# A fourth weight buffer for the experts, and scatters that add into a running sum in memory

## The reference: what is computed

```python
def hier_moe(h, w_rg, b_rg, w_re, b_re, w_eg, w_eu, w_ed):
    ...                       # softmax over 4 groups, the best group g_sel; 8 experts in it, the best 2
    weights = pg_top * pe_top                      # (T, 2)
    gidx = g_sel * EXPERTS_PER_GROUP + e_sel       # both experts of a token are in one group
    ...
    for e in range(N_EXPERTS):                     # 32 experts, FF = 256
        a = jax.nn.silu(h @ w_eg[e]) * (h @ w_eu[e])
        out = out + gate[:, e:e + 1] * (a @ w_ed[e])
    return out
...
hm = rmsnorm(x, norm_moe)
x = x + hier_moe(hm, ...)
return rmsnorm(x, norm_final)
```

## Time and profile before

| | |
|---|---|
| median of 3 runs | 1280.27 us (1277.06 to 1283.28) |
| the profiled execution | 1284.23 us, its span 1282.5 us |
| the experts' tiles | about 921 to 1244 us of the span |
| the end behind them | 1244 to 1282.5 us |
| PE busy | 1185.2 us, 92% of the span |
| moved by DMA | 184.53 MB, of these 100.7 MB expert weights (96 loads of 1 MB) |

### The profile page before, as it was taken

How to read it: one execution, slowest core, us unless ns; L and a number is a source line. 1 busy time by engine, 2 the same in 40 slices (tenths; PEclk the granted TensorE clock), 3 DMA queues, 4 the chain that set the end, 5 groups by cost and what they waited for, 6 DMA issues and landing times.

```text
span 1282.5 us, 18554 instructions
## 1 busy us (share of the span) xinstructions
PE 1185.2 (92%) x7302; PEld 1070.8 (83%) x7302; DVE 643.9 (50%) x1057; ACT 602.7 (47%) x998; POOL 331.8 (26%) x225
## 2 busy tenths in 40 slices
PE   7999999998999999999999999999699999999960
PEld 6999899888878878899999999999687887777750
DVE  4201512436653443355302021435788998888857
ACT  5333644645644444133212213123477887787843
POOL 0221112123203111131112023210244465444520
PEclk9999999998999999999999999999799999999995
DMA  6441101124102021112121222501889999999817
GB/s 221 166 140 34 33 14 42 51 78 120 50 1 68 1 66 34 34 46 60 47 66 42 66 75 66 186 34 39 332 319 374 365 363 348 369 351 363 338 61 295
DMA packets 93575, 184.53 MB, mean 144 GB/s; under 512 B 17385, under 2 KB 68989, under 8 KB 85310
## 3 DMA queue, kind: packets, MB, share of 16 engines
q1 hardware_dynamic: 82606, 167.43, 36.9%
q0 software_dynamic: 10896, 16.08, 3.5%
HBM read 179.72 MB, written 28.65 MB: 162 GB/s over the span
## 4 chain that ended last, share of the span: by engine, by line
PE 71%; ACT 9%; DVE 8%; DMA 6%; issue 4%; SPq 0%; POOL 0%; POOLq 0%; ACTq 0%; DVEq 0%
PE bank L1297 11%; PE bank L1299 11%; PE bank L1298 11%; DMA raw_gu<-in_w_exp_up 5%; PE bank L1364 5%; PE bank L1365 5%; PE bank L1366 5%; PE bank L1498 3%; PE bank L1500 3%; PE bank L1499 3%; PE bank L1445 2%; PE bank L1376 2%; ACT w_hi L1041 1%; PE bank L1398 1%; PE bank L1485 1%
## 5 line engine op out<-in xcount | busy, mean ns | idle before, releaser
L913 POOL TENSOR_TENSOR w_lo<-raw,w_hi 128x2048 fp32r<-128x2048 f32 (+2 forms) x34 | 140.6, 4136 | 598.2 <-ACT w_hi L1041 453.0
L1297 PE MATMUL bank<-hT_hi,w_hi 128*128 128x384 f32 (+1 forms) x592 | 202.6, 342 | 2.5 <-POOL w_lo L913 1.8
L1299 PE MATMUL bank<-hT_hi,w_lo 128*128 128x384 f32 (+1 forms) x592 | 199.6, 337 | 0.0
L1298 PE MATMUL bank<-hT_lo,w_hi 128*128 128x384 f32 (+1 forms) x592 | 199.4, 337 | 0.0
L1931 DVE TENSOR_TENSOR lo_gu<-raw_gu,hi_gu 128x2048 fp32r<-128x2048 f32 x64 | 146.3, 2287 | 4.7 <-ACT hi_gu L1030 4.5
L1030 ACT ACTIVATE hi_gu<-raw_gu 128x2048 fp32r<-128x2048 f32 x64 | 122.5, 1918 | 51.0 <-issue 51.0
L1364 PE MATMUL bank<-w_hi,hT_hi 128*128 128x256 f32 x432 | 124.8, 289 | 0.0
L1365 PE MATMUL bank<-w_lo,hT_hi 128*128 128x256 f32 x432 | 122.1, 283 | 0.0
L1366 PE MATMUL bank<-w_hi,hT_lo 128*128 128x256 f32 x432 | 122.1, 283 | 0.0
L1297 PEld LDWEIGHTS bank<-hT_hi,w_hi 128*128 128x128 f32 (+1 forms) x592 | 112.1, 189 | 6.3 <-issue 5.2
L1298 PEld LDWEIGHTS bank<-hT_lo,w_hi 128*128 128x128 f32 (+1 forms) x592 | 112.1, 189 | 0.3
(11 more groups left out here) (301 smaller groups left out, 2626.0 us busy)
## 6 DMA issues: line engine op xcount, KB each, us to landing
raw_gu<-in_w_exp_gate SPq DMA_DIRECT2D x32, 1024.0 KB, 11.2
raw_gu<-in_w_exp_up SPq DMA_DIRECT2D x32, 1024.0 KB, 13.7
raw_down<-in_w_exp_down SPq DMA_DIRECT2D x32, 1024.0 KB, 15.4
raw<-in_w_in SPq DMA_DIRECT2D x25, 1024.0 KB, 5.6
y_pair<-y_d SPq DMA_DIRECT2D x12, 512.0 KB, 8.5
raw<-in_w_in SPq DMA_DIRECT2D x8, 512.0 KB, 5.5
raw<-in_w_proj_b SPq DMA_DIRECT2D x4, 1024.0 KB, 5.1
raw<-in_w_out SPq DMA_DIRECT2D x4, 1024.0 KB, 5.6
```

Source lines behind the costliest of these rows:

```text
L913: pool.tensor_tensor(w_lo[:, g % 2, 0:kb, 0:n], raw[:, g % 2, 0:kb, 0:n], w_hi[:, g % 2, 0:kb, 0:n].bitcast(F32), ALU.subtract).then_inc(w ...
L1297: pe.matmul(out, l_hi, r_hi, start=j == 0, stop=False)
L1298: pe.matmul(out, l_hi, r_lo, start=False, stop=False)
L1299: ins = pe.matmul(out, l_lo, r_hi, start=False, stop=j == n - 1)
```

## The change

`WRING` is 4: a fourth gate/up buffer and a fourth down buffer stand where `x1` stood (140 to 164 KB of a partition). The loop becomes 2 turns of 12 tiles, since 12 is a multiple of the 4 buffers and the 2 places. `x1` moves to memory: as soon as a tile of tokens has its final x1, SP stores it to `sum_d` (768 x 1024). The result of an expert is scaled by the pair's weight on ACT as it leaves PE's accumulator, and the scatter adds it to the token's row of `sum_d`. For this the table now has a slot's row index alone (`slot_x`) and its weights (`slot_w`), which come from a wider float32 matmul (`w_hot`, 56 columns where there were 24) in the place of the overflow table. Since both experts of a token lie in one group, the tiles take the groups in turn (0, 8, 16, 24, 1, 9, ...), so that two scatters in flight never add to one row. At the end SP loads 6 tiles of `sum_d` and not 12 of `y_d`, and the products and sums of L1991 are gone.

```diff
-WRING = 3
+WRING = 4
...
-        gu_raw = [at(f"raw_gu{r}", [P, 2, KD, FF], F32, kb) for r, kb in enumerate((8, 24, 104))]
+        gu_raw = [at(f"raw_gu{r}", [P, 2, KD, FF], F32, kb) for r, kb in enumerate((8, 24, 104, 140))]
...
-        y_pair = at("y_pair", [P, NT, 2, D], F32, 8)
+        x_sum = at("x_sum", [P, NT, D], F32, 8)
...
-        LOOPED = 4
-        FIRST, TURN = 2, 2 * WRING
+        LOOPED = 2
+        FIRST, TURN = 2, 12
...
+        def expert_at(i, g, n):
+
+            return (g + n) % NGRP * EPG + i + (g + n) // NGRP
...
+                if s.kind == "h2T" and s.half == 0:
+
+                    evac_done(sp, E_, find(kind="ts", dest=("out", 3), i=s.i)[0].job)
+                    sp.dma_start(sum_d[s.i * P:(s.i + 1) * P, :], x1[:, s.i, :]).then_inc(x1_out, 16)
...
-            load(kinds[0:2], 2, 2, 2)
-            sp.wait_ge(over_mm, 1)
+            load(kinds[0:2], expert_at(0, 0, 2), 2, 2)
+            sp.wait_ge(x1_out, 16 * NT)
+            sp.wait_ge(h2_out, 16 * NT)
+            load(kinds[0:2], expert_at(0, 0, 3), 3, 3)
+            sp.wait_ge(w_mm, 1)
+            load(kinds[2:3], expert_at(0, 0, 2), 2, 2)
...
             for i in range(NT):
-                for j in range(2):
-                    sp.dma_start(y_pair[:, i, j, :], y_d[j * T + i * P:j * T + (i + 1) * P, :]).then_inc(pair_in[i], 16)
+                sp.dma_start(x_sum[:, i, :], sum_d[i * P:(i + 1) * P, :]).then_inc(sum_in[i], 16)
...
-            def scatter(e, p, k):
+            def scatter(e, p, k, ring, slot):
...
                     pool.wait_ge(y_out[p], k * 16)
...
+                pool.tensor_copy(y_idx[:, p:p + 1], slot_x[:, bass.ds(slot, 1)]).then_inc(y_copied, 1)
+                pool.tensor_copy(y_w[:, p:p + 1], slot_w[:, bass.ds(slot, 1)]).then_inc(y_copied, 1)
+                pool.wait_ge(y_copied, e * 2 + 2)
                 pool.wait_ge(y_done, e + 1)
                 pool.sem_inc(y_ready, 1)
-                pool.indirect_dma_start(y_d, bass.IndirectOffsetOnAxis(ap=y_idx[:, p:p + 1].bitcast(U32), axis=0),
-                                        m_y[:, p, :], None, bounds_check=2 * T - 1, oob_is_err=False).then_inc(y_out[p], 16)
+                pool.indirect_dma_start(sum_d, bass.IndirectOffsetOnAxis(ap=y_idx[:, p:p + 1].bitcast(U32), axis=0),
+                                        m_y[:, p, :], None, bounds_check=T - 1, oob_is_err=False,
+                                        compute_op=ALU.add).then_inc(y_out[p], 16)
...
+            pool.wait_ge(y_out[1], NE // 2 * 16)
             n_over = beyond(pool, beyond_tile)
             pool.wait_ge(y_out[0], (n_over + NE // 2) * 16)
-            pool.wait_ge(y_out[1], NE // 2 * 16)
...
+                act.wait_ge(y_copied, e * 2 + 2)
...
+                    ins = act.activation(m_y[:, p, half * 512:(half + 1) * 512], psum[B_Y[half]][:, :], ACT.Copy,
+                                         scale=y_w[:, p:p + 1])
...
-                ins = pe.matmul(psum[B_Y[0]][:, 0:2 * OEVEN], row_hot[:, j, :], over_hot[:, j, :, :].rearrange("p a n -> p (a n)"),
+                ins = pe.matmul(psum[B_AT[1]][:, 0:LATE], row_hot[:, j, :].bitcast(F32), w_hot[:, j, :],
...
-                        ins = dve.scalar_tensor_tensor(x1[:, i, :], y_pair[:, i, j, :], pair_w[:, i, j:j + 1], x1[:, i, :],
-                                                       ALU.mult, ALU.add)
```

More of the change, by code:

```diff
@@ L533, in build @@
         h2_d = nc.dram_tensor("h2_d", (T, D), F32, kind="Internal").ap()
-        y_d = nc.dram_tensor("y_d", (2 * T, D), F32, kind="Internal").ap()
+        sum_d = nc.dram_tensor("sum_d", (T, D), F32, kind="Internal").ap()
         def sem(name):
@@ L821, in _ @@
             need(sp, E_, mm, last_out + 1)
-            load(kinds, 0, 0, 0)
-            load(kinds, 1, 1, 1)
+            load(kinds, expert_at(0, 0, 0), 0, 0)
+            load(kinds, expert_at(0, 0, 1), 1, 1)
             sp.wait_ge(mm, len(jobs.by))
@@ L828, in _, with tile @@
             sp.wait_ge(x_gathered[0], 16)
[L829 to L832 removed]
+            load(kinds[0:2], expert_at(0, 0, 2), 2, 2)
[4 more added lines that the diff above has]
+            load(kinds[2:3], expert_at(0, 0, 2), 2, 2)
+            def tile(e, p, k, r, u, i, g):
                 if ahead(e, WRING):
[L834 removed]
+                    load(kinds[0:2], expert_at(i, g, WRING), e + WRING, r)
                 if ahead(e, WRING - 1):
[L836 removed]
+                    load(kinds[2:3], expert_at(i, g, WRING - 1), e + WRING - 1, later(r, u, WRING - 1)[0])
             first_tiles(sp.Fori, tile)
@@ L1237, in hi_a, with result @@
                    .then_inc(at_hi, 1)
-            def result(e, p, k):
+            def result(e, p, k, ring):
                 act.wait_ge(y_mm, e + 1)
-                if not (isinstance(k, int) and k == 0):
+                act.wait_ge(y_copied, e * 2 + 2)
+                if not (isinstance(e, int) and e < ring):
                     act.wait_ge(y_out[p], k * 16)
                 for half in range(2):
-                    ins = act.activation(m_y[:, p, half * 512:(half + 1) * 512], psum[B_Y[half]][:, :], ACT.Copy)
+                    ins = act.activation(m_y[:, p, half * 512:(half + 1) * 512], psum[B_Y[half]][:, :], ACT.Copy,
+                                         scale=y_w[:, p:p + 1])
                 ins.then_inc(y_done, 1)
@@ L1249, in _, with tile @@
             hi_x(1, 1, 2)
-            def tile(e, p, k, r, u):
+            def tile(e, p, k, r, u, i, g):
                 silu(e, p, 2)
@@ L1255, in tile @@
                 if not first(e):
-                    result(e - 1, 1 - p, k - (1 - p))
+                    result(e - 1, 1 - p, k - (1 - p), 2)
                 if ahead(e, 2):
@@ L1265, in _ @@
             first_tiles(act.Fori, tile)
-            result(NE - 1, 1, NE // 2 - 1)
+            result(NE - 1, 1, NE // 2 - 1, 2)
             def beyond_tile(e, j, k, u):
@@ L1273, in beyond_tile @@
                 hi_a(e, 0, 1)
-                result(e, 0, k)
+                result(e, 0, k, 1)
             beyond(act, beyond_tile)
             for i in range(NT):
-                act.wait_ge(sum_done, i + 1)
-                act.activation(junk3[:, :], x1[:, i, :], ACT.Square, accum_out=ss[:, i:i + 1]).then_inc(sq3, 1)
+                act.wait_ge(sum_in[i], 16)
+                act.activation(junk3[:, :], x_sum[:, i, :], ACT.Square, accum_out=ss[:, i:i + 1]).then_inc(sq3, 1)
                 act.wait_ge(sq3, i + 1)
@@ L1514, in down @@
                 pe.wait_ge(w_lo_done["down"], e + 1)
-                if isinstance(e, int) and e == 0:
-                    pe.wait_ge(over_evac, 1)
-                else:
+                if not (isinstance(e, int) and e == 0):
                     pe.wait_ge(y_done, e)
@@ L1856, in _ @@
                     ins.then_inc(hot_done, 1)
-                    mark(dve.tensor_tensor(slot_hot[:, of(b), :, :], twice(pairs(hot)[:, of(b), :], NE),
-                                           across(pairs(iota_xy)[:, of(b), :], NE), ALU.mult))
+                    mark(dve.tensor_tensor(slot_hot[:, of(b), :], pairs(hot)[:, of(b), :], spread(iota_x[:, sl, :], NE), ALU.mult))
                     if b == 1:
@@ L1960, in _, with tile @@
             lo_x(1, 1)
-            overflow_table()
+            late_table()
             lo_weights("back", 1, 1, 1)
-            def tile(e, p, k, r, u):
+            def tile(e, p, k, r, u, i, g):
                 gated(e, p, 2)
```

130 lines of the change are left out of this document (66 added, 64 removed).

## The result

| | before | after |
|---|---|---|
| median | 1281.58 us (1277.06 to 1283.28, 4 runs) | 1302.14 us (1301.21 to 1304.1, 4 runs) |
| ratio, 95% interval | | 1.0175 [1.0151, 1.0199] |
| the profiled execution | 1284.23 us | 1302.26 us, its span 1300.5 us |
| last scatter starts | 1244.16 us | 1271.73 us |
| first load of the results | 1249.87 us | 1282.38 us |

The change costs 1.75%: the forecast was 1297 us, and 1302.14 were measured. The three stretches add up: +27.6 us to the last scatter, +4.9 from there to the first load (10.65 instead of 5.71), -14.4 at the end (15.06 instead of 29.52). That is +18.1, and the profiled executions are 18.0 apart.

What follows compares the result with a forecast made beforehand. The busiest DMA engine was taken to bound the tiles; +27.5 us to the last scatter and -10.8 at the end gave +16.7, so 1280.3 became 1297 us; 8-in-10 range 1256 to 1320, the forecast's own 1286 to 1313.

Steps and rivals of the forecast that it cites:

- The bound: Expert tiles: the DMA engines carrying rows never rest and the others wait; the slowest engine needs 9.9 us a tile.
- the rival of 1256 us: Expert tiles: latency is the limit and PE becomes the bound at 9.28 us a tile; chance 0.13.
- The adding row: Scatters in the tiles: an adding row takes twice a plain one, 0.32 us, adding 1.15 us a tile.
- The rivals of 1265 (hidden read), 1281 and 1329 (round trip): Scatters: an adding row costs 0.16 us (chance 0.17), 0.24 us (0.10), or 0.48 us and more (0.15).
- The chain of 28 tiles: Tiles 4 to 31 on the slowest engine, 11.05 us each: last scatter at 1272 against 1244.2, +27.5 us.
- The head start at plain cost: Expert tiles with the fourth buffer and plain-cost adding rows: last scatter at 1239.9, -4.3 us.
- Ahead of the loop: Before the tiles: the wider float32 matmul takes 2.8 us against 1.4 and delays DVE, +1.5 us.
- The order: Expert tiles: taking experts by groups moves no work and leaves a tile's cost the same.
- POOL: Tiles: one more POOL copy, 0.2 us, stays hidden; 0, up to 1 us a tile if landing took 14.
- The end (a): After the last scatter: the beyond loop waits for its landing instead of its issue, +2.7 us.
- The end (b): From SP's first load of results to the last output tile: 16.0 us instead of 29.5, -13.5 us.
- PE's clock: Tiles: taken as 1.00 throughout; the forecast would be too low if it fell in longer waits.

Runs made afterwards that it cites:

- e2: Kernel before with each expert's rows placed so that consecutive ranks go to different DMA engines; 1267.88 us, ratio 0.9904.
- e1: Kernel after with plain scatters that write rows instead of adding them (outputs not the reference's); 1265.78 us, ratio 0.9904.
- e7: Kernel after with each adding scatter replaced by two plain ones, to sum_d and a second tensor; 1298.83 us, ratio 1.0140.
- e10: e1 (plain scatters) with three weight buffers instead of four; 1274.76 us, ratio 0.9962.
- e11: Kernel before with the experts taken in turn from the four groups; 1282.24 us, ratio 1.0015.
- e12: Kernel after with POOL's y_w copied early and the wait for the last scatters moved behind the beyond loop, rows not spread; 1295.67 us, ratio 1.0120.
- e3: Kernel after with rows spread over the DMA engines as in e2; 1268.00 us, ratio 0.9912.
- e5: e3 with POOL copying y_w ahead of its index copy and gather; 1259.28 us, ratio 0.9828.
- e6: e5 with POOL's wait for the last scatters moved behind the beyond loop; 1252.94 us, ratio 0.9792.
- e9: e6 with three weight buffers instead of four; 1255.61 us, ratio 0.9810.

## Why the prediction was right, point by point

- **The bound.** Right, and shown by e2: the busiest engine, not latency (the rival of 1256 us is refuted by the kernel after itself, and in e2 by PE's 9.28 us with three buffers). Engine or way into memory is not told apart (above).
- **The adding row**, forecast at 0.32 us and 1.15 us a tile. Right in the row: 0.327 us in the packet records. In the tile 11.24 us in the last sixteen and 11.10 in the last 13, where 11.05 stood; against e1's 9.86 the last 13 give 1.24 a tile. The rivals of 1265 (hidden read), 1281 and 1329 (round trip) are out, e7 against the last. The 0.19 us over in the last sixteen may be of another kind, below.
- **The chain of 28 tiles.** The last scatter was forecast for 1272 and came at 1271.73, less 1.6 us for a profile that reached the router sooner (below). That it fits to 0.3 us is in part luck. The way there is different from the text: PE did the first ten tiles on the head start, at 9.28 us but for the first (10.44, as before) and two of 10.95, while the engines fell behind, and waited only then.
- **The head start at plain cost**, -4.3 us. From the gate load of tile 2 (913.55 in e1) to the last scatter (1234.54) e1 takes 321.0 us and the kernel before 324.6 (919.60, 1244.16): -3.6; e10, with three buffers, takes 324.2.
- **Ahead of the loop**, +1.5. Right: the 12 matmuls take 2.78 us, where 2.8 stood (12 x 0.24 is 2.9), and from the router's last matmul group (898.01 us; 899.58 in the earlier trace rows) to the product of tile 1 (941.16; 941.12 in the earlier trace rows) it takes 1.6 us longer. The stretch before that was 1.6 us shorter in this profile.
- **The order**, 0. Right (e11).
- **POOL**, 0 to 1 us a tile. The step that failed is "queued behind are its scatter and its next gather", which left the copy at its shortest length. It is long when DVE's split runs, and it stands behind the gather. Two tiles of 10.95 us in the kernel after; there it costs next to nothing (e12), but 8.7 us once the engines have room (e3, e5).
- **The end (a)**, +2.7. Mis-sized: +4.9. Two sizes were off, by 1.2 and 1.1 us. By its last semaphore update in the trace the last scatter landed after 4.8 us, not 3.6. And from there to the first load it took 5.9 us, where 4.7 lay between the end of the issue and the load before (5.71 less 0.97). e1 shows the second without the add: its last scatter lands after 2.6 us as before, and its first load starts 8.43 us after the scatter (1234.54, 1242.97). The place of the wait cost 5.0 us in the kernel after (e12), 3.9 with spread rows (e6). **The end (b)**, -13.5: -14.4.
- **PE's clock.** The text warned of it and took 1.00. It was 0.96 in the sixteen late tiles, and 0.50 from 1133 to 1137 us, the lower of its two levels (1.2 GHz). PE's timeline of the kernel after, around it:

```profile
1129.37 0.39 PE L1524 MATMUL bank<-lo_gu,m_xT_hi 128*128 128x512 f32 x1
1132.64 0.79 PE L1321 MATMUL bank<-hi_down,m_aT_hi 128*128 128x512 f32 x1 [2.88 <-DVE m_aT_lo L1977]
1133.23 0.63 PE L1322 MATMUL bank<-lo_down,m_aT_hi 128*128 128x512 f32 x1
...
1137.92 0.63 PE L1522 MATMUL bank<-hi_gu,m_xT_hi 128*128 128x512 f32 x1
...
1138.95 0.40 PE L1522 MATMUL bank<-hi_gu,m_xT_hi 128*128 128x512 f32 x1
```

From the gap of 2.88 us to 1138.4 the same matmul of 512 columns takes 0.63 us, and they start 0.43 us apart instead of 0.23. PE was busy 158.0 us in sixteen tiles that take 16 x 9.28 = 148.5 when it never waits: 9.5 us. Not all of it is the clock's: before, with waits but at 1.00, the 27 tiles show 255.73 us of busy time, and 251.07 in e2, without waits. How much of it is on the path and how much only fills waits for weights was not tried and stays open; the tile's 0.19 us above the forecast leave room for 3 us in sixteen tiles.

The sum came to +16.7 and the profiles are 18.0 apart. The errors are small and partly cancel: the end (a) 2.2 us too low, the end (b) 0.9 too high. The forecast of 1297 is 5.1 us below the median of 1302.14, and most of that is no term of the sum: 3.9 us were taken off because the profiled execution before stood above its median, while that of the kernel after, 1302.26, stands at its median; the median before rose to 1281.58 with a fourth run.

Slips of the prediction that moved little: by a ratio of 1.93 the sum would be 2 us lower (0.07 x 1.15 x 28), not 1; and a row of 0.28 us gives 1289 (28 x 7.2 x 0.12 = 24, less 4.3 and 10.8), not 1286, the lower end of the forecast's own range.

## What to carry to other kernels

Where DMA is near the bound, look at the busiest of the 16 engines and not at their mean share: 0.95 with stretches at half the rate was a full engine here, and placing a tile's rows over all partitions, at no cost in bytes, was worth 1.0% before the change and 2.6% after it. One more buffer does not make a full engine faster: it gave a head start once (3 to 4 us in the profiles with plain scatters). Price an adding scatter at two plain ones, and let it land beside other work. With rows spread, the weight copied early and the end's wait moved (e6) the idea of the change gives 0.9792 of the kernel before, 1252.94 us, and hardly needs the fourth buffer for it (e9: 0.9810). Spreading the rows alone gives 0.9904 (e2), so about half of that gain belongs to the adding scatters, and it lies in the end, which they shorten by 14.4 us.

## What the runs showed of the hardware that I had not expected

- A POOL copy of 128 values takes 0.17 us alone and 2.25 us beside a DVE instruction of 2.28 us; POOL's own part in issuing a gather goes from 1.05 to 2.67 us in such tiles, and that of an adding scatter from 1.60 to 3.35. Any POOL instruction that another engine waits for needs that much slack.
- Issuing an adding scatter keeps POOL for 1.56 us at the least, a plain one for 0.97.
- After a wait of PE of 2.9 us the granted clock stood at 0.50, the lower level, for 5.8 us; in the kernel before, with waits of up to 1.09 us, it never left 1.00 in the tiles. The length of the last wait alone doesn't decide it. Three windows of the kernel after follow: the first stands behind a wait of 2.78 us and stays at 1.00, the second behind one of 1.80 us (0.56), the third behind one of 2.83 us (0.50).

```profile
1041.00:1044.00 3.00, 2.92 (x13) 2.43 (x14) 2.45 (x4) 2.61 (x4) 2.15 (x4) 1.00 1.01 352
1087.00:1090.50 3.50, 3.50 (x11) 2.69 (x9) 3.31 (x3) 2.22 (x3) 2.68 (x2) 0.56 0.99 400
1186.80:1189.60 2.80, 2.80 (x7) 2.23 (x8) 2.30 (x3) 2.54 (x3) 1.95 (x4) 0.50 1.04 410
```
